# Feed-forward gate and up tiles of a hybrid attention block: seven products of 2x2 blocks in place of eight

## The reference

```python
f = rms_norm(h, norm_ffn_pre[l])
f = (jax.nn.silu(f @ w_ffn_gate[l]) * (f @ w_ffn_up[l])) @ w_ffn_down[l]
h = h + rms_norm(f, norm_ffn_post[l])
```

## Time and profile before

| | |
|---|---|
| median of 3 runs | 851.03 us (849.64 to 851.29) |
| the profiled execution, its own time | 850.82 us |
| its span in the profile | 848.9 us |
| PE busy | 831.8 us, 98% |
| DVE busy | 465.5 us, 55% |
| ACT busy | 364.7 us, 43% |
| POOL busy | 104.3 us, 12% |
| granted TensorE clock, mean | 0.998 of full speed |

### The profile page before, as it was taken

One profiled execution on the slowest core, in us unless ns is written; L12 is line 12 of the kernel. 1 busy time (PEld: TensorE's weight loads), 2 busy tenths in 40 slices (PEclk: granted clock), 3 DMA queues, 4 the chain that ended last, 5 costly groups with the idle time before them and its releaser, 6 DMA issues.

```text
span 848.9 us, 17488 instructions
## 1 busy us (share of the span) xinstructions
PE 831.8 (98%) x7429; PEld 694.5 (82%) x7429; DVE 465.5 (55%) x592; ACT 364.7 (43%) x544; POOL 104.3 (12%) x106
## 2 busy tenths in 40 slices
PE   6999999999999999999999999999999999999997
PEld 5999999876778777678888988888888888888886
DVE  5459998433858576296675744444444444322333
ACT  6445665427474855653453533333223333211231
POOL 2015434200403122233000000000000000000000
PEclk9999999999999999999999999999999999999999
DMA  9232232321111111331677123333333333333311
GB/s 287 83 94 75 75 91 84 124 74 44 59 47 53 42 53 52 107 93 59 193 226 241 50 75 99 99 99 99 99 98 89 92 96 96 99 100 100 112 61 75
DMA packets 109579, 82.57 MB, mean 97 GB/s; under 512 B 3471, under 2 KB 100025, under 8 KB 109258
## 3 DMA queue, kind: packets, MB, share of 16 engines
q1 hardware_dynamic: 109514, 81.61, 31.5%
HBM read 75.83 MB, written 5.77 MB: 96 GB/s over the span
## 4 chain that ended last, share of the span: by engine, by line
PE 91%; DVE 5%; ACT 2%; issue 1%; POOL 0%; DMA 0%; DVEq 0%; SPq 0%; POOLq 0%
PE psum L582 49%; PE psum L1816 19%; PE psum L1613 6%; PE psum L1554 6%; PE psum L1859 2%; PE psum L1446 2%; DVE w_lo L572 1%; PE psum L1755 1%; PE psum L1767 1%; PE psum L1736 1%; DVE shift_diff L1151 1%; PE psum L1437 1%; DVE k_mod L1192 1%; DVE v_t L1156 1%; PE psum L1521 1%
## 5 line engine op out<-in xcount | busy, mean ns | idle before, releaser
L572 DVE TENSOR_TENSOR w_lo<-w_raw,w_hi 128x1024 fp32r<-128x1024 f32 x69 | 87.9, 1276 | 116.5 <-ACT w_hi L567 112.1
L582 PE MATMUL psum<-f_hi,w_hi 128*128 128x512 f32 x336 | 130.8, 389 | 0.0
L582 PE MATMUL psum<-f_lo,w_hi 128*128 128x512 f32 x336 | 130.7, 389 | 0.0
L582 PE MATMUL psum<-f_hi,w_lo 128*128 128x512 f32 x336 | 130.7, 389 | 0.0
L1392 DVE TENSOR_TENSOR w_lo<-w_raw,w_hi 128x1024 fp32r<-128x1024 f32 x44 | 53.9, 1226 | 125.6 <-ACT w_hi L1063 121.4
L1063 ACT ACTIVATE w_hi<-w_raw 128x1024 fp32r<-128x1024 f32 x44 | 46.7, 1061 | 166.6 <-PE psum L582 159.4
L567 ACT ACTIVATE w_hi<-w_raw 128x1024 fp32r<-128x1024 f32 x70 | 73.8, 1055 | 71.8 <-PE psum L1816 56.0
L582 PE MATMUL psum<-h_hi,w_hi 128*128 128x264 f32 (+2 forms) x400 | 98.2, 310 | 0.8 <-DVE w_lo L572 0.8
L582 PE MATMUL psum<-h_lo,w_hi 128*128 128x264 f32 (+2 forms) x400 | 96.5, 306 | 0.0
L582 PE MATMUL psum<-h_hi,w_lo 128*128 128x264 f32 (+2 forms) x400 | 96.5, 306 | 0.0
L582 PEld LDWEIGHTS psum<-f_hi,w_lo 128*128 128x128 f32 x336 | 63.1, 188 | 13.2
(11 more groups left out here) (287 smaller groups left out, 1557.4 us busy)
## 6 DMA issues: line engine op xcount, KB each, us to landing
w_raw<-in_w_in SPq DMA_DIRECT2D x30, 512.0 KB, 3.7
w_raw<-in_w_g SPq DMA_DIRECT2D x22, 512.0 KB, 3.6
w_raw<-in_w_u SPq DMA_DIRECT2D x22, 512.0 KB, 3.7
w_raw<-in_w_d SPq DMA_DIRECT2D x22, 512.0 KB, 3.6
w_raw<-in_w_in SPq DMA_DIRECT2D x48, 128.0 KB, 2.2
w_raw<-in_w_out SPq DMA_DIRECT2D x8, 512.0 KB, 5.3
kept_gates<-gate_raw SPq DMA_DIRECT2D x10, 256.0 KB, 2.3
sig_t<-kept_gates SPq DMA_DIRECT2D x10, 256.0 KB, 2.9
```

Of the source, the lines that this page charges most:

```text
L572: nc.vector.tensor_sub(lo[:], raw[u % RAW][:], hi[:].bitcast(F32)).then_inc(w_split, 1)
L582: mm = nc.tensor.matmul(o, w[:, (w0 + i) * P:(w0 + i + 1) * P], xs[:, k, c0:c1], start=(n == 0), stop=(n == total - 1))
```

## The change

The first 4 of the 22 pairs (`PLAIN = 4`) stay as they were, written out without the loop. The other 18 (`SEVENS`) are computed as the product of a 2x2 block matrix by a 2x2 block matrix in Winograd's form. The left matrix has the rows gate and up and the columns "first four 128-row blocks" and "last four": a11, a12, a21, a22. The right one is the activation, split by the same halves of the 1024 rows and by the first and last 256 tokens: b11, b12, b21, b22. Eight block products become seven (`FACTORS`), each of 4 blocks of 128 x 128, 3 matmuls each of 256 columns. The left factors are a11, a12, a22 and four sums s1 to s4, which POOL makes for each pair; the right factors are b11, b21, b22 and t1 to t4, which are made once, while the plain pairs run. The seven products go through 4 half buffers of `w_hi` and `w_lo` (`SLOTS`). Products 3, 5 and 6 of a pair are added in PSUM to earlier ones; ACT copies the earlier sums out first (`p1`, `u2`, `p5`, `u3`), and DVE adds the copies back (`c11`, `c12`, `c22`, `c21`).

```diff
+SUMS = ("s2", "s1", "s3", "s4")
+FACTORS = (("a11", "b11"), ("a12", "b21"), ("s2", "t2"), ("s1", "t1"), ("s3", "t3"), ("s4", "b22"), ("a22", "t4"))
+SLOTS = 4
+SEVEN_ACT = by_slot([[(0, "hi"), (1, "sig")], [(0, "p1"), (0, "hi")], [(0, "hi")], [(0, "u2"), (0, "hi"), (1, "round")],
+                     [(0, "p5"), (0, "hi")], [(0, "u3"), (0, "hi")], [(0, "hi")]])
+SEVEN_DVE = by_slot([[(1, "c21"), (0, "lo")], [(1, "silu"), (0, "lo")], [(0, "c11"), (1, "act"), (0, "lo")],
+                     [(0, "lo"), (1, "rest")], [(0, "lo")], [(0, "lo")], [(0, "c12"), (0, "c22"), (0, "lo")]])
...
+            for j in range(SEVENS):
+                if j < 2:
+                    sp.wait_ge(w_split, U_DOWN + 2 * j - 2)
+                else:
+                    sp.wait_ge(factor_split, 7 * (j - 1))
+                for i, w in enumerate((w_g, w_u)):
+                    sp.dma_start(pair_raw(j)[i][:].rearrange("p (k n) -> p k n", k=KT), tile_of(w, PLAIN + j)
+                                 ).then_inc(pair_in[j % 2], 16)
...
+            for name in ("b12", "b11", "b22", "b21"):
+                g.tensor_tensor(quarter_of(f_sum, name), quarter_of(f_hi, name).bitcast(F32), quarter_of(f_lo, name).bitcast(F32),
+                                ALU.add).then_inc(f_whole, 1)
+            for j, t in SEVEN_POOL:
+                if j:
+                    pool.wait_ge(factor_split, 7 * (j - 1) + [name for name, _ in FACTORS].index(t) + 1)
+                if t == "s1":
+                    g.tensor_tensor(sums[t][:], a21, a22, ALU.add).then_inc(s_made, 1)
+                if t == "s2":
+                    g.tensor_tensor(sums[t][:], sums["s1"][:], a11, ALU.subtract).then_inc(s_made, 1)
+                if t == "s3":
+                    g.tensor_tensor(sums[t][:], a11, a21, ALU.subtract).then_inc(s_made, 1)
+                if t == "s4":
+                    g.tensor_tensor(sums[t][:], a12, sums["s2"][:], ALU.subtract).then_inc(s_made, 1)
...
+            def seven_hi(m):
+                    act.wait_ge(factor_used, m - SLOTS + 1)
+                s_.activation(factor(m)[0], factor_of(m), ACT.Copy).then_inc(factor_hi, 1)
...
+            def seven_lo(m):
+                dve.wait_ge(factor_hi, m + 1)
+                v_.tensor_sub(lo, factor_of(m), hi.bitcast(F32)).then_inc(factor_split, 1)
...
+                if step == "c11":
+                    dve.wait_ge(factor_used, 7 * j + 2)
+                    dve.wait_ge(side_act, side(SIDE_ACT, j, "p1"))
+                    v_.tensor_tensor(ffn_t[0][:, low], bank(b + 1, 256), old_a, ALU.add).then_inc(side_dve, 1)
+                if step == "c22":
+                    v_.tensor_tensor(ffn_u[1][:, high], old_a, old_c[:], ALU.add).then_inc(side_dve, 1)
+                if step == "silu":
+                    v_.tensor_mul(ffn_t[1][:], ffn_t[0][:], ffn_t[1][:]).then_inc(side_dve, 1)
+                if step == "act":
+                    v_.tensor_mul(ffn_u[1][:], ffn_u[1][:], ffn_t[1][:]).then_inc(side_dve, 1)
...
+            def seven(m):
+                j, n = divmod(m, 7)
+                pe.wait_ge(factor_split, m + 1)
+                if n in (2, 4, 5):
+                    pe.wait_ge(side_act, side(SIDE_ACT, j, {2: "p1", 4: "u2", 5: "p5"}[n]))
+                for k in range(KT // 2):
+                    rows_hi, rows_lo = rows_of(FACTORS[n][1], k)
+                    for i, (w, xs) in enumerate(((hi, rows_hi), (hi, rows_lo), (lo, rows_hi))):
+                        mm = t_.matmul(bank(b, 256), w[:, k * P:k * P + P], xs, start=(n in (0, 1, 3, 6) and k == 0 and i == 0),
+                                       stop=(k == KT // 2 - 1 and i == 2), skip_group_check=True)
+                mm.then_inc(factor_used, 1)
```

More of the change, by code:

```diff
@@ L501, in build @@
         f_sig = sem("ffn_sig")
+        f_whole = sem("ffn_rows_whole")
+        t_made = sem("row_sums_made")
+        t_hi_done = sem("row_sums_hi")
+        t_lo_done = sem("row_sums_lo")
+        pair_in = [sem(f"pair_landed{i}") for i in range(2)]
+        s_made = sem("weight_sums_made")
+        factor_hi = sem("factor_hi")
+        factor_split = sem("factor_split")
+        factor_used = sem("factor_used")
+        side_act = sem("seven_act")
+        side_dve = sem("seven_dve")
         stored = sem("stored")
@@ L554, in split @@
                 return o_hi[u - U_OUT - SPL], o_lo[u - U_OUT - SPL]
+            if u == U_DOWN:
+                return down_hi, down_lo
             if U_HELD <= u < N_UNITS - SPL:
@@ L566, in hi_unit @@
                 act.wait_ge(w_used, u - HELD + 1)
+            if u == U_DOWN:
+                act.wait_ge(factor_split, 7 * SEVENS - 1)
+            if u == U_DOWN + 1:
+                act.wait_ge(factor_used, 7 * SEVENS - 2)
             nc.scalar.activation(split(u)[0][:], raw[u % RAW][:], ACT.Copy).then_inc(w_hi_done, 1)
@@ L1051, in _ @@
             hi_unit(act, U_FFN + 2)
[L1052 to L1063, removed]
@@ L1064, in _ @@
-            for k in range(3, FT):
+            def seven_hi(m):
+                if m < 2:
+                    act.wait_ge(w_used, U_DOWN - 1)
+                elif m < SLOTS:
+                    act.wait_ge(w_used, U_DOWN)
+                else:
+                    act.wait_ge(factor_used, m - SLOTS + 1)
+                name = FACTORS[m % 7][0]
+                if name[0] == "a":
+                    pair_landed(act, m // 7)
+                else:
+                    act.wait_ge(s_made, side(SEVEN_POOL, m // 7, name))
+                s_.activation(factor(m)[0], factor_of(m), ACT.Copy).then_inc(factor_hi, 1)
@@ new lines, in _ @@
+            for m in range(3):
+                seven_hi(m)
+            for n, j, step in SEVEN_ACT:
+                m = 7 * j + n
+                b = first_bank(j)
+                if step == "hi" and m + 3 < 7 * SEVENS:
+                    seven_hi(m + 3)
+                    if m == 0:
+                        act.wait_ge(w_used, U_DOWN)
+                        act.wait_ge(t_made, 1)
+                        s_.activation(quarter_of(f_hi, "b12"), t_sum[0][:], ACT.Copy).then_inc(t_hi_done, 1)
+                if step == "hi" and 7 * SEVENS <= m + 3 < 7 * SEVENS + 2:
+                    hi_unit(act, U_DOWN + m + 3 - 7 * SEVENS)
+                if step == "p1":
+                    act.wait_ge(factor_used, 7 * j + 1)
+                    if j:
+                        act.wait_ge(side_dve, side(SIDE_DVE, j - 1, "c21"))
+                    else:
+                        act.wait_ge(tail_dve, FFN_AT + (PLAIN - 1) * len(TAIL_FFN))
+                    s_.activation(old_a, bank(b, 256), ACT.Copy).then_inc(side_act, 1)
+                if step == "u2":
+                    act.wait_ge(factor_used, 7 * j + 3)
+                    if j:
+                        act.wait_ge(side_dve, side(SIDE_DVE, j - 1, "c12"))
+                    s_.activation(old_b, bank(b, 256), ACT.Copy).then_inc(side_act, 1)
+                if step == "p5":
+                    act.wait_ge(factor_used, 7 * j + 4)
+                    if j:
+                        act.wait_ge(side_dve, side(SIDE_DVE, j - 1, "c22"))
+                    s_.activation(old_c[:], bank(b + 2, 256), ACT.Copy).then_inc(side_act, 1)
+                if step == "u3":
+                    act.wait_ge(factor_used, 7 * j + 5)
+                    act.wait_ge(side_dve, side(SIDE_DVE, j, "c11"))
+                    s_.activation(old_a, bank(b, 256), ACT.Copy).then_inc(side_act, 1)
+                if step == "sig":
+                    act.wait_ge(side_dve, side(SIDE_DVE, j, "c12"))
+                    if j:
+                        act.wait_ge(side_dve, side(SIDE_DVE, j - 1, "act"))
+                    else:
+                        act.wait_ge(tail_dve, LAST_AT)
+                    s_.activation(ffn_t[1][:], ffn_t[0][:], ACT.Sigmoid).then_inc(side_act, 1)
+                if step == "round":
+                    act.wait_ge(side_dve, side(SIDE_DVE, j, "act"))
+                    s_.activation(act_hi[:, PLAIN + j, :], ffn_u[1][:], ACT.Copy).then_inc(side_act, 1)
@@ L1065, in _ @@
+            for k in range(2, FT):
                 hi_unit(act, U_DOWN + k)
@@ L1384, in _ @@
             out_lo(3)
[L1386 to L1407, removed]
@@ L1822, in activated @@
                 if k == 0 and b == 2:
-                    pe.wait_ge(tail_dve, FFN_AT + (FT - 2) * len(TAIL_FFN))
+                    pe.wait_ge(tail_dve, LAST_AT)
+                    pe.wait_ge(side_dve, side(SIDE_DVE, SEVENS - 2, "rest"))
                 if k == 0 and b == 0:
-                    pe.wait_ge(tail_dve, LAST_AT)
+                    pe.wait_ge(side_dve, len(SIDE_DVE))
             pe.wait_ge(gate_out, 2 * KT)
```

218 lines of the change are left out of this document (194 added, 24 removed).

## The result

The changed kernel takes 859.86 us (median of 4 runs, 859.31 to 861.63) against 851.16 us for the kernel before, run beside it (median of 4): ratio 1.0109, interval 1.0089 to 1.0129. It is slower by 8.7 us; the forecast was 863.2 us, slower by 12. The span of the profiled execution is 857.6 us, 8.7 us above that of before.

The account below looks back on a forecast made before the run. PE bounded the kernel before; DVE, taking turns with POOL, was to bound the changed pairs at 11.7 us against 10.89. 15 pairs gave +12.2 us on 850.82, 863.0, plus 0.2 for the median: 863.2 us, range 849 to 877.

Parts of the forecast that it names:

- PE: Matmuls of the 18 changed pairs: 84 of 256 columns at 0.1205 us, 10.12 us a pair, 0.77 us less than before.
- DVE's own steps: DVE in a changed pair: ten steps at 0.61 us and four at 0.33 us, 7.42 us in all.
- The holds: DVE and POOL take turns on SBUF operands in changed pairs: each POOL sum costs DVE 1.09 us, 4.36 us a pair.
- The overlap with `c11`: In each changed pair only c11, of the steps reading PSUM, runs beside a POOL sum: 0.2 us taken off.
- the 0.1 us for waits between engines: Added to DVE's 11.6 us in a changed pair, making 11.7 us.
- The ends: First two changed pairs live on the lead, last pair runs at about PE's own pace: 0 each.
- PE as the bound: Rival for the changed pairs: DVE and POOL steps pass each other, PE stays the bound, 838 us; chance 0.12.
- The prediction's condition for it: PE bounds the changed pairs once DVE's round falls under 10.12 us: three of four holds must vanish or nearly so.
- The lock on the shared ports: Skill's wording for DVE and POOL, held the whole instruction: a sum costs 1.23 us, a pair 12.2 us, 871 us.
- Break-even: Rival: sums drift beside c12, c22 and c21, DVE at 10.8 to 11.0 us a pair, 849 to 853 us; chance 0.08.
- a queue standing still: Rival: DVE's queue also waits on ACT in changed pairs, 0.7 us more, 12.4 us a pair, 874 us; chance 0.20.

Follow-up runs that it names:

- without sums: Changed kernel with POOL making the four weight sums for the first changed pair only, the other 17 pairs reusing them: 836.6 us, ratio 0.984.
- the fill of SBUF that reads nothing: Changed kernel with POOL filling the four sum tiles with a constant from the second changed pair on, same waits: 838.3 us in a single run.
- the run with late sums: Changed kernel, all work done, s3 and s4 waiting longer, to start when DVE reaches c12 and c21: 856.45 us, ratio 1.0064.

## Why the prediction was right

It held in direction, in cause and, within 3.3 us, in size. The size is in part luck: the pair was put 0.28 us too long and the entry at nothing, and these two errors work against each other. By its steps:

- **PE.** 84 matmuls of 256 columns were put at 0.1205 us and 10.12 us a pair, from 264 and 250 columns. Measured without sums: 0.1198 us and 10.06 us. The gain that was to be had on PE was there: 10.89 - 10.06 = 0.83 us a pair.
- **DVE's own steps.** Forecast 7.42 us, measured 7.35 (0.60 us in place of 0.61 from start to start).
- **The holds.** Forecast 1.09 us for a sum, from two turns in the earlier trace rows; measured 1.11, 1.10 and 1.09. The reading of the trace before carried over to a stretch where POOL had never worked.
- **The overlap with `c11`.** This was the mis-sized term. I took off 0.2 us; in 16 of the 18 pairs (those whose `act` step takes 1.45 us) s1's hold begins within 0.1 us of `c11` and covers it, 0.33 us (1.10 - 0.77). The rest of the 0.28 is the 0.1 us for waits between engines, of which nothing was there, and the 0.07 of DVE's own steps. So the pair came to 11.42 us and not 11.7, 0.28 x 15 = 4.2 us less.
- **The ends.** I had put entry and exit at nothing. From the first matmul of 256 columns to the down product it is 732.46 - 528.63 = 203.8 us, against 18 x 10.89 = 196.0 before: +7.8, which is 15 x 0.53 within 0.2. The entry cost 2.4 us besides. To read it, both traces are taken from the last group of eight small matmuls ahead of the plain pairs (`z_tok`), which starts at 486.84 before and at 485.42 after. Before, the 6 units that follow end at 495.02 + 144 x 0.2268 = 527.68 by the earlier trace rows, 140.8 us after that group; after, the first matmul of 256 columns starts at 528.63, 143.2 us after it. PE waits there for `w_lo` at 493.90 (0.29 us), 521.97 (0.56) and 528.63 (0.92). The first wait falls beside POOL's `f_sum`, the other two follow DVE's t sums and a `w_lo`, which met POOL's first weight sums. One of these t sums on DVE's timeline:

```profile
512.86 2.35 DVE L1613 TENSOR_TENSOR t_sum<-f_sum 128x1024 f32<-128x1024 f32 x1
```

PE's timeline at the first matmul of 256 columns:

```profile
528.63 0.38 PE L2185 MATMUL psum<-f_hi,w_hi 128*128 128x256 f32 x1 [0.92 <-DVE w_lo L1592]
```

and the chain's step of the down product:

```profile
732.46 12.55 PE psum L2097 x55
```

Together +10.2 us. The profiled execution of the changed kernel had come to that group 1.4 us earlier than the one of before, which is scatter from execution to execution: the traces of the experiments have it between 485.45 and 487.79. That leaves 8.8 us, the change of the span (8.7).

The rivals: PE as the bound was wrong for this kernel and came true at once, at 836.6 to 837.6 us (838 forecast), when the holds were gone. The prediction's condition for it, three of four holds gone or nearly so, was too strict: by its own terms 11.7 - 2 x 1.09 = 9.5 us is under 10.12, and with two holds left the run took 836.9 us. Break-even came true when the sums were laid beside `c12` and `c21`. Of a queue standing still there was no sign: DVE is busy for 159.9 of 160 us. The Trainium skill (TensorE: Matmul & The Clock Gate, Part 1) states a start-to-start for matmuls by which the estimate is 109 ns for 256 columns. No run here met it: the lowest average is 119.8 ns. The lock on the shared ports that the Trainium skill states (SBUF — State Buffer, "SBUF: two separate sides") is what the trace shows, with the loser's start-up, some 0.14 us, done during its wait; and the fill of SBUF that reads nothing took no turn.

What stays open: s1 mostly loses a turn. It is issued at 622.25, while DVE's `silu` runs until 622.73, but DVE's `w_lo`, issued at 622.65, goes first, and s1's hold begins only at its end. s2, issued at 613.21 with as much of DVE's step left (0.41 us), gets the next turn. It isn't the kind of step either: in the run with late sums s1 is issued as long before the end of `silu` (0.47 us) and goes first. POOL's line there, and DVE's `w_lo` that waits for it:

```profile
610.47 1.63 POOL L896 TENSOR_TENSOR sum_s<-w_raw 128x512 f32<-128x512 f32 x1 [0.68 <-DVE w_lo L1592]
610.86 1.78 DVE L1592 TENSOR_TENSOR w_lo<-sum_s,w_hi 128x512 fp32r<-128x512 f32 x1
```

No run here tells what decides it. In the changed kernel the slip costs nothing and is what brings s1 beside `c11`.

## What to carry to other kernels

Before an idle engine is given work, ask what it shares with the busy ones: here each elementwise step on GpSimd that reads SBUF held back VectorE's next step with two operands in SBUF for 1.15 us, and where VectorE is near the bound that is dearer (1.1 us net) than the step on VectorE itself (0.6 us). Look for the price in the trace of before, in the ends of two instructions of the two engines that overlap. It costs nothing while the loser stays under the next bound, and beside steps that read PSUM part of it (0.33 us a step here) can be hidden, if the other engine already stands waiting when they begin.

## What the runs showed of the hardware

- DVE and POOL alternate one instruction at a time when both have two operands in SBUF: 1.15 to 1.16 us for POOL's 128 x 512 and 0.55 us for DVE's, to and fro (timelines of the changed kernel). The one exception is the turn that s1 loses.
- A POOL step of 128 x 512 with two operands that is released when nothing holds it takes 1.30 us; one that already waits takes 1.15 us from the other's end. The same for DVE: 0.68 and 0.55 us.
- A DVE step of two operands of which one is in PSUM kept its 0.41 us beside a sum, and a POOL fill of 0.53 us beside a DVE step of two SBUF operands changed neither.
- DVE's step need not have two operands in SBUF to be held. In the plain pairs of the changed kernel the rounding `act_hi`, with one operand, takes 1.12 us in place of 0.43, while POOL's `f_sum` runs until 499.45; the two steps before it, with an operand in PSUM, keep 0.68 and 0.69 us. Five of the experiments show the same 1.11 or 1.12 us there. From the timelines of DVE and POOL:

```profile
498.62 1.12 DVE L1607 TENSOR_SCALAR act_hi<-ffn_u 128x512 fp32r<-128x512 f32 x1
492.72 6.73 POOL L883 TENSOR_TENSOR f_sum<-f_hi,f_lo 128x1024 f32<-128x1024 f32 x2
```

- Matmuls of 128 x 128 by 256 columns, each with its own weight load, start 0.1198 us apart on average, 0.2268 us for 512 columns: halving the columns gives 0.53 of the time, so seven products of two halves cost 7/8 x 1.056 = 0.92 of eight, and not 0.875.
